# Scores of two heads issued in turn on the two row halves of TensorE, in a kernel of two attention layers, two mixers and a gathered expert stage

## The reference, cut to what matters

```python
for l in range(2):
    proj = rms_norm(x, norm_g[l]) @ w_in[l]
    # per query tile of 128 rows, per head (g, i), head size 64:
    s_c = q @ kc.T ; s_s = q @ ks.T ; s_w = q @ kw.T      # three score matrices
    out = g0*softmax(s_c)@vc + g1*softmax(s_s)@vs + g2*softmax(s_w)@vw
    x = x + concat(out*silu(z), lru, conv) @ w_out[l]
# second block: latent attention (4 heads, 128 plain + 64 rotated columns), mLSTM (4 heads of 64), then experts
s = (q_nope @ k_nope.T + q_rope @ k_rope.T) * scale
x = x + gate * (concat(softmax(s) @ v, mlstm) @ w_out)
x = x + gate2 * sum_k w_k * gelu(u_k . h) * v_k           # rows u_k, v_k gathered from 16384 experts
```

## Time and profile before

| | |
|---|---|
| median of 3 runs | 1511.21 us (1508.91 to 1512.95) |
| the profiled execution | 1515.22 us, span 1513.8 us |
| PE busy | 1083.6 us (72%) |
| DVE busy | 920.6 us (61%) |
| ACT busy | 350.8 us (23%) |
| scores of heads, `bank<-kT,qT` | 128 MATMUL records |
| layers' attention | about 96 to 266 us and 357 to 528 us |
| mixers, tile 0 | 715.5 to 745.7 us |
| expert stage | from about 770 us to the end |

### The profile page before, as it was taken

How to read it: one execution, slowest core, us unless ns; L and a number is a source line. 1 busy time by engine, 2 the same in 40 slices (tenths; PEclk the granted TensorE clock), 3 DMA queues, 4 the chain that set the end, 5 groups by cost and what they waited for, 6 DMA issues and landing times.

```text
span 1513.8 us, 17204 instructions
## 1 busy us (share of the span) xinstructions
PE 1083.6 (72%) x6241; PEld 624.0 (41%) x6241; DVE 920.6 (61%) x2431; ACT 350.8 (23%) x816; POOL 281.4 (19%) x260
## 2 busy tenths in 40 slices
PE   7997999999799949998966777665443444433434
PEld 4775655577665514643652443133222211211100
DVE  5488523348752332834546668867777776776765
ACT  2014313101431220245522542232110111111100
POOL 0000000000000000000012324344444343444440
PEclk9998999999799958998977989796666667556666
DMA  7443442454344051217119869999999999999996
GB/s 277 159 163 139 149 162 94 165 197 132 134 167 166 1 209 36 82 56 262 48 61 392 342 230 415 422 418 376 420 420 419 421 419 420 420 420 420 411 409 282
DMA packets 111350, 391.10 MB, mean 258 GB/s; under 512 B 10907, under 2 KB 39118, under 8 KB 78498
## 3 DMA queue, kind: packets, MB, share of 16 engines
q0 software_dynamic: 36864, 268.45, 43.0%
q1 hardware_dynamic: 74402, 121.56, 22.8%
HBM read 387.89 MB, written 1.05 MB: 257 GB/s over the span
## 4 chain that ended last, share of the span: by engine, by line
DMA 19%; PE 15%; DVE 13%; POOL 8%; ACT 4%; issue 4%; another core or an unknown queue 1%; DVEq 0%; ACTq 0%; SPq 0%
DMA e_uv<-in_experts_dram,e_listed 17%; PE bank L169 14%; POOL e_uv L2903 8%; DVE e_uv L2696 4%; DMA e_w_pq<-in_w_pq_dram 2%; ACT L229 1%; PE bank L174 1%; ACT e_h2q L229 1%; ACT m_W L229 1%; DVE m_W L185 1%; DVE e_hT L192 1%; DVE e_hot L185 0%; DMA e_h2q<-in_final_g_dram 0%; DVE e_diag L185 0%
## 5 line engine op out<-in xcount | busy, mean ns | idle before, releaser
L2903 POOL DMA_INDIRECT e_uv<-in_experts_dram,e_listed x256 | 281.2, 1099 | 1196.9 <-DVE e_listed L202 1005.3
L169 PE MATMUL bank<-e_uv,e_diag 128*32 128x512 f32 x1024 | 240.9, 899 | 313.5 <-DVE e_diag L185 294.8
L2696 DVE CUSTOM_DVE_ANT_0 e_uv<-e_uv,e_h2q 128x1024 f32<-128x1024 f32 x192 | 229.5, 1221 | 75.6 <-DMA e_uv<-in_experts_dram,e_listed 60.4
L169 PEld LDWEIGHTS bank<-e_uv,e_diag 128*32 128x32 f32 x1024 | 42.6, 141 | 446.9 <-DVE e_diag L185 336.9
L169 PE MATMUL bank<-hT,weights 128*128 128x256 f32 x640 | 151.2, 400 | 10.4 <-DVE fb L197 8.8
L169 PEld LDWEIGHTS bank<-hT,weights 128*128 128x128 f32 x640 | 128.0, 201 | 30.1 <-DVE fb L197 8.9
L169 PE MATMUL bank<-weights,hT 128*128 128x512 f32 (+1 forms) x256 | 102.6, 557 | 2.5 <-DMA weights<-in_w_in_dram 2.5
L229 ACT ACT_TABLE_LOAD x74 | 94.9, 1283 | 13.7 <-PE bank L169 9.0
L197 DVE SCALAR_TENSOR_TENSOR conv<-ubuf,vec,conv 128x256 f32<-128x256 f32 x240 | 96.8, 479 | 0.6
L169 PE MATMUL bank<-weights,mixT 128*128 128x512 f32 x192 | 88.6, 615 | 2.4 <-DVE mixT L202 1.6
L229 ACT ACTIVATE e_act<-e_dot 128x4 f32<-128x4 f32 (+2 forms) x84 | 17.2, 204 | 300.1 <-DVE e_dot L2696 298.1
(11 more groups left out here) (375 smaller groups left out, 1461.3 us busy)
## 6 DMA issues: line engine op xcount, KB each, us to landing
weights<-in_w_in_dram SPq DMA_DIRECT2D x16, 2048.0 KB, 7.7
weights<-in_w_ada_dram SPq DMA_DIRECT2D x8, 2048.0 KB, 7.8
weights<-in_w_out_dram SPq DMA_DIRECT2D x6, 2048.0 KB, 7.7
e_w_pq<-in_w_pq_dram SPq DMA_DIRECT2D x12, 1024.0 KB
weights<-in_cmp_w_dram SPq DMA_DIRECT2D x4, 2048.0 KB, 7.9
m_w<-in_w_in_dram SPq DMA_DIRECT2D x2, 2048.0 KB, 11.7
m_wo<-in_w_ada_dram SPq DMA_DIRECT2D x2, 2048.0 KB, 8.9
m_w<-in_w_ada_dram SPq DMA_DIRECT2D x2, 2048.0 KB, 9.6
```

Of the source, the lines that this page charges most:

```text
L169: ins = self.engine.matmul(out, lhsT, rhs, start=start, stop=stop, **kw)
L2696: dve.mark(c.nc.vector.tensor_tensor_reduce(u, u, h2q[tt][n], 1.0, 0.0, MUL, ADD, m["dot"][:, j:j + 1]), ("dots_set", g, c0) if n == c1 - ...
L2903: ins = c.nc.gpsimd.indirect_dma_start(out=m["uv"][j], out_offset=None, in_=A["experts"], in_offset=bass.IndirectOffsetOnAxis(ap=of, axis=0))
```

## The change

It lets each TensorE call issue two heads: the scores of g = 0 and g = 1 of one i are taken and issued together at the even unit's step, matmuls alternating between the row halves and written to two banks. Compressed scores alternate in the same way. Because pairs must be neighbours, the compressed unit moves from place 5 to 6 of a tile (units 6 and 15). In the mixers' first tile `att_scores` takes two heads: their two 128 row products follow each other, then their two rotated products, one on each row half. Heads 0 and 1 stand before the loop, 2 and 3 behind `levels(2)`. In the expert stage `att_scores` is still called with one head. VectorE's and ScalarE's functions are unchanged, but for the moved unit.

```diff
-    UNITS.insert(len(UNITS) - 2 * REP + 5, ("compressed", qt_, 0, 0))
+    UNITS.insert(len(UNITS) - 2 * REP + 6, ("compressed", qt_, 0, 0))
...
-    def scores(u, qt, i, g):
+    def scores(u, qt, i):
+
         nk = (qt + 1) * P
-        bank = take("scores", l, u)
+        banks = [take("scores", l, u + g) for g in range(KV)]
         for b in range(2):
-            pe.mm(bank[:, b * T:b * T + nk], qT[g * HD:g * HD + HD, i, qt * P:qt * P + P],
-                  kT[g * HD:g * HD + HD, b, 0:nk], tell=filled("scores", l, u) if b else None)
+            for g in range(KV):
+                pe.mm(banks[g][:, b * T:b * T + nk], qT[g * HD:g * HD + HD, i, qt * P:qt * P + P],
+                      kT[g * HD:g * HD + HD, b, 0:nk], tell=filled("scores", l, u + g) if b else None)
 
     def compressed_scores(u, qt):
         pe.wait_ge(*c.taken("kcT", l))
-        for g in range(KV):
-            bank = take("c_scores", l, u, g)
-            for i in range(REP):
-                pe.mm(bank[:, i * CMP_PAD:(i + 1) * CMP_PAD], qT[g * HD:g * HD + HD, i, qt * P:qt * P + P],
+        banks = [take("c_scores", l, u, g) for g in range(KV)]
+        for i in range(REP):
+            for g in range(KV):
+                pe.mm(banks[g][:, i * CMP_PAD:(i + 1) * CMP_PAD], qT[g * HD:g * HD + HD, i, qt * P:qt * P + P],
...
-            if kind == "head":
-                scores(step, qt, i, g)
-            else:
+            if kind == "compressed":
                 compressed_scores(step, qt)
+            elif g == 0:
+                scores(step, qt, i)
...
-    tile.att_scores(0)
+    tile.att_scores(0, 1)
     for h in range(MLA_H):
         if h + 1 < MLA_H:
             tile.levels(h + 1)
-            tile.att_scores(h + 1)
+            if h == 1:
+                tile.att_scores(2, 3)
             tile.lstm_scores(h + 1)
...
-    def att_scores(self, h):
+    def att_scores(self, *heads):
+
         c, m, tt = self.c, self.m, self.tt
-        bank = c.banks.take("att_scores", tt, h)
...
+        banks = [c.banks.take("att_scores", tt, h) for h in heads]
+        for bank, h in zip(banks, heads):
+            c.pe.mm(bank[:, :], self.s["qnT"][:, h, :], m["knT"][:, h, :], start=True, stop=False)
+        for bank, h in zip(banks, heads):
+            side = slice((h % 2) * ROPE2, (h % 2) * ROPE2 + ROPE2)
+            c.pe.mm(bank[:, :], m["qrT"][side, h // 2, tt * P:tt * P + P], m["krT"][side, h // 2, :], start=False, stop=True,
+                    tell=c.banks.filled("att_scores", tt, h))
```

## The result

The changed kernel takes 1517.17 us (median of 7 runs), the kernel before 1512.59 (7 runs): ratio 1.0031, 95% interval 1.0022 to 1.0040, so 4.6 us slower. The profiled execution took 1518.14 us, its span is 1516.7. TensorE is busy 1064.8 us instead of 1083.6: 19 us of its work are gone, and the end is later.

The account below looks back on a forecast made before the run. It took TensorE to bound the layers' second query tile and mixers' tile 0, DMA from 770 us; layer 0 +3.35, layer 1 -0.7 and mixers +5.1, say +7.7, moved 1511.2 to 1518.9 us, range 1511.5 to 1524.0.

Parts of the forecast that it names:

- The sign: Whole kernel: slower by more than 4.5 us at 0.59, within that at 0.32, faster at 0.09.
- A pair costs 1.07 us: Layers: two heads' scores overlap fully, 1.07 us in the second query tile, 0.65 in the first.
- Step 3: Layers, lru_gate's second bank: waits for VectorE's read of unit 3, covered by the hidT wait; 0, bounds -1.3 to +1.2.
- Steps 5 to 14: Layer 0: zc 0 +0.8; running shift +1.3 at 188.8, +1.6 at out12 (0,0), +0.55 at step 12, -0.15 at ada 3.
- Step 17: Layer 0, out12 (1,1): waits 3.0 us for unit 17's bank; shift +1.25, clock 2.1; layer 1's out12 starts earlier.
- Layers together: Both layers: +3.35 in layer 0 (1.25 plus 2.1 for the clock), -0.7 in layer 1 (-1.2 plus 0.5).
- Mixers: Tile 0: att_turned(2) waits 3.2 us for att_scores(3)'s bank; +2.7, clock 2.1 and 0.3, together +5.1.
- The clock did drop: Against a rival: same waits, but the clock stays up or falls elsewhere, +0.2 to +4, middle 1513.5 us; chance 0.25.
- Rival 3: Layers and mixers: banks free at the takes or VectorE earlier, 12.3 us off, net -10.7, 1500.5 us; chance 0.08.

Follow-up runs that it names:

- The last experiment: Changed layers, old mixers, five passes without the one ahead of lru_gate's second bank: 1479.42 us, ratio 0.9798 to the kernel before.
- the last two kernels: Kernel before with one bank passed over ahead of zc 0 in each layer (0.9884), and the kernel of The last experiment (0.9798).
- five passes: Changed layers, old mixers, banks passed over ahead of layer 0's out12 (1,1) and each layer's lru_gate second bank, zc 0, out12 (0,0), ada 3: 0.9849 to before.

## Why the prediction came out as it did

Forecast: 1518.9 us, range 1511.5 to 1524.0; measured 1517.17, and 4.6 us of loss for a forecast of 7.7. The sign and the main mechanism, TensorE waiting for banks, were right; the layers' part of the sum was not. That the total came so close is partly luck: the layers came out 4.4 us below their terms and the mixers 1.7 us above theirs, and the kernel before measured 1.4 us more in the runs of the comparison than in those I started from.

- **A pair costs 1.07 us.** Right (1.06, and 0.64 in the first tile), and the row of the compressed unit was a good guide, though I misread it a little: its counts are of records that run in the stretch, and of the ten only eight start in it, which is still over twice the rate. The Trainium skill's rule on the order of matmuls (TensorE: Matmul & The Clock Gate, Part 3) asks that they start and end in program order; eight records in 1.07 us, issued head by head, disagree with it again, since the second head's first ones must start beside the first head's first.
- **Step 3.** I charged 0 with bounds -1.3 and +1.2. It came out below the lower bound in both layers: first scores to vc takes 45.35 and 45.00 us with the old layers and 43.40 to 43.73 with the new (layer 1: 46.31 and 45.82, against 43.74 to 44.10). The stop makes lru_gate late, where hidT hides it, and zlru 2 runs at full clock behind it (7.17 us for 9.23). This is the mis-sized term: -1.7 and -2.1 us by the means, where the sum had 0. The last experiment, with the stop back, confirms it.
- **Steps 5 to 14.** The order of takes was right at all five places (these three, lru_gate and step 17), and the stops stand where it put them: zc 0 (6.64 us for 4.38), out12 (0,0) at 199.05 (forecast 199.3), ada 3 (0.58). The list was right for "what does the change add"; it was blind for what was there before, since I took zc 0's wait as given.
- **Step 17.** The stop before out12 (1,1) of layer 0 was forecast as 3.0 us (2.51), none in layer 1 (none). The clock price behind it was forecast as 2.1 and was 2.0 between the two profiled executions, but that is not the change's: in the other profile of the old layers out12 (1,1) takes 9.58 us too. Over the profiles of the table it is 9.5 us after (mean of four) against 8.3 (mean of two, 6.97 and 9.58), which is too few to size the term. In layer 1 it is 8.1 us (mean of four) against 6.97 in both old ones, 1.1 us for the 0.5 that I had for the clock there.
- **Layers together:** forecast +2.65, measured -1.8 (interval -3.5 to -0.2). Step 3 is 3.8 of the 4.4 us between. The rest is small only in sum: by the means of the table the stretch behind layer 1, where I had nothing, is 1.2 us shorter, and layer 1 without its step 3 is 0.3 longer where I had 0.7 shorter; layer 0 without its step 3 is 3.2 longer for a forecast of 3.35, which may be chance, as two executions of its old code differ by 3.7.
- **Mixers:** forecast +5.1 in the tile. The tile measured +5.4: the stop before att_values(0) put it at 728.54 (forecast 728.0 plus the 0.58 by which the tile starts later), att_turned(2) stood 3.79 us (3.2), 2.65 us were the clock's (2.1). In the median it is 6.8, with an interval from 4.5 to 8.9.
- **Rivals.** The clock did drop. Rival 3's 12.3 us, if banks are free, is near what the last two kernels differ by (13 us, without the mixers' 2.2, but with step 3's gain and more banks passed over). That the two figures lie close shows nothing by itself. But its place of decision, the released bank at the take, was the right one.

## What to carry to other kernels

A rotation of PSUM banks is a schedule of waits of its own: write out which earlier reader each take waits for, and for every stop ask whether the instruction needs data or only a bank. Where it is only the bank, handing out another adds no instruction. Here it was worth 29 us (0.9798 against 0.9988), six times what the pairing had lost, and the largest stop had been there before the order was touched. Try each place by itself: one of the five passes cost 7.7 us, and the new order of banks in the mixers moved the stop one head on. And compare a stretch of the same code in two executions before a microsecond of it is put down to a change.

## What the runs showed of the hardware

- Matmuls on different row halves overlap fully even when all of one head's (four records) are issued ahead of the other's: 1.07 us for both. With eight records a head (16 columns each) only a part does: 1.46 us, against 1.00 in turn.
- Such overlap also comes unplanned. levels (36 rows) and lstm_scores of an odd head (64 rows on the upper half), issued next to each other by the change, interleave: records of both start in turn from 738.07 and 738.09 on, and from levels(3) to the end of lstm_scores(3) it is some 0.4 us less than one behind the other.
- One stop can buy a full clock later: lru_gate's pause, hidden behind another engine, left zlru 2 at 2.4 GHz (7.17 us) in both layers of every profile that has the pause; in those without it, the two of the old layers, the old order with one bank passed over and the five passes, it takes 8.9 to 10.1 us. Why the clock falls in just these stretches was not tried.
- A stop filled with idle matmuls keeps the clock at 1.00 behind it (outputs(2) 1.73 us instead of 3.22).
